# Two groups' scatters ahead of two units in a sparse-expert build stage

## The reference, cut to what matters

```python
def peer_ffn(x, w_q, sub_keys, u, v):
    ...
    s1, i1 = lax.top_k(s[..., 0, :], PEER_TOPK)
    s2, i2 = lax.top_k(s[..., 1, :], PEER_TOPK)
    ...
    cand_i = (i1[..., :, None] * PEER_NKEYS + i2[..., None, :])
    top_s, pos = lax.top_k(cand_s, PEER_TOPK)
    gate = jax.nn.softmax(top_s, axis=-1)
    ...
        hid = jnp.einsum('thkd,td->thk', u[ib], xb)
        a = jax.nn.gelu(hid.astype(jnp.float32), approximate=False) * gb
        return jnp.einsum('thk,thkd->td', a.astype(x.dtype), v[ib])
```

## Time and profile before

| | |
|---|---|
| median of 3 runs | 1659.34 us (1658.65 to 1662.34) |
| profiled execution | 1656.8 us, span 1655.0 us |
| busy in the span | PE 1623.7 (98%), PEld 1484.2 (90%), DVE 1034.1 (62%), ACT 978.3 (59%), POOL 1128.9 (68%) |
| chain that ended last | PE 85%, POOL 6%, issue 3%, DVE 3%, ACT 2%, DMA 1% |
| build stage | first scatter at 1131.74 us, late stage from 1325.68 us |

### The profile page before, as it was taken

How to read it: one execution, slowest core, us unless ns; L and a number is a source line. 1 busy time by engine, 2 the same in 40 slices (tenths; PEclk the granted TensorE clock), 3 DMA queues, 4 the chain that set the end, 5 groups by cost and what they waited for, 6 DMA issues and landing times.

```text
span 1655.0 us, 30488 instructions
## 1 busy us (share of the span) xinstructions
PE 1623.7 (98%) x10334; PEld 1484.2 (90%) x10334; DVE 1034.1 (62%) x2292; ACT 978.3 (59%) x1972; POOL 1128.9 (68%) x897
## 2 busy tenths in 40 slices
PE   8999999999999999999999999999999999999999
PEld 7888888889998888799998999988999999999998
DVE  2785432334343332746443398986999988889997
ACT  5556655556465555665653667675555566666665
POOL 8455799998989999887655699997899811111210
PEclk9999999999999999999999999999999999999999
DMA  6333455555555555554352466665777788889995
GB/s 235 102 104 113 153 188 184 187 189 168 189 166 190 190 187 186 165 174 129 130 188 90 141 199 207 203 224 196 238 250 254 249 290 284 271 303 312 333 344 174
DMA packets 104318, 334.38 MB, mean 202 GB/s; under 512 B 12144, under 2 KB 26608, under 8 KB 103952
## 3 DMA queue, kind: packets, MB, share of 16 engines
q1 hardware_dynamic: 94368, 294.99, 53.2%
q0 software_dynamic: 9696, 37.91, 7.7%
q10 hardware_dynamic: 144, 0.08, 0.0%
HBM read 324.90 MB, written 7.47 MB: 201 GB/s over the span
## 4 chain that ended last, share of the span: by engine, by line
PE 85%; POOL 6%; issue 3%; DVE 3%; ACT 2%; DMA 1%; SPq 0%; POOLq 0%; DVEq 0%; ACTq 0%
PE bank L777 21%; PE bank L809 18%; PE bank L1438 10%; PE bank L810 9%; POOL w_lo L685 6%; PE banks_and L777 6%; PE bank L1440 5%; PE banks_and L1438 3%; PE bank L1415 2%; PE banks_and L1440 2%; PE bank L755 1%; PE banks_and L1327 1%; PE banks_and L1415 1%; DMA ring<-stream 1%; ACT w_hi L1493 1%
## 5 line engine op out<-in xcount | busy, mean ns | idle before, releaser
L685 POOL TENSOR_TENSOR w_lo<-ring,w_hi 128x512 fp32r<-128x512 f32 x804 | 1041.8, 1313 | 237.7 <-ACT w_hi L1493 202.8
L1493 ACT ACTIVATE w_hi<-ring 128x512 fp32r<-128x512 f32 x1060 | 663.3, 630 | 527.8 <-PE bank L810 248.0
L809 PE MATMUL bank<-h_high_and_low,w_hi 128*128 128x448 f32 (+1 forms) x1728 | 583.5, 389 | 2.0 <-POOL w_lo L685 1.9
L810 PE MATMUL bank<-h_high_and_low,w_lo 128*128 128x224 f32 (+1 forms) x1728 | 467.5, 271 | 0.0
L809 PEld LDWEIGHTS bank<-h_high_and_low,w_hi 128*128 128x128 f32 x1728 | 325.1, 188 | 52.5 <-POOL w_lo L685 3.9
L810 PEld LDWEIGHTS bank<-h_high_and_low,w_lo 128*128 128x128 f32 x1728 | 328.8, 190 | 1.6
L1438 PE MATMUL bank<-A_high_and_low,w_hi 128*128 128x448 f32 x768 | 256.6, 375 | 1.6 <-ACT mask_parts L1968 1.6
L777 PE MATMUL bank<-h_high_and_low,w_hi 128*128 128x256 f32 x1312 | 249.1, 288 | 2.2 <-POOL w_lo L685 1.7
L777 PEld LDWEIGHTS bank<-h_high_and_low,w_hi 128*128 128x128 f32 x1312 | 209.7, 194 | 4.9 <-issue 2.6
L1440 PE MATMUL bank<-A_high_and_low,w_lo 128*128 128x224 f32 x768 | 202.0, 263 | 0.0
L2827 DVE TENSOR_TENSOR w_lo<-ring,w_hi 128x512 fp32r<-128x512 f32 x256 | 176.2, 689 | 27.5 <-ACT w_hi L1493 16.0
(11 more groups left out here) (447 smaller groups left out, 2360.5 us busy)
## 6 DMA issues: line engine op xcount, KB each, us to landing
ring<-stream SPq DMA_DIRECT2D x530, 512.0 KB, 3.6
spill<-mask_parts SPq DMA_DIRECT2D x56, 112.0 KB, 2.8
XN<-spill SPq DMA_DIRECT2D x56, 112.0 KB, 6.1
arena<-branch_w POOLq DMA_DIRECT2D x1, 3072.0 KB, 12.7
X<-x SPq DMA_DIRECT2D x2, 512.0 KB, 4.4
arena<-kv_w SPq DMA_DIRECT2D x1, 1024.0 KB, 6.0
out<-X SPq DMA_DIRECT2D x4, 256.0 KB, 2.1
arena<-row POOLq DMA_DIRECT2D x1, 512.0 KB, 4.8
```

The costliest lines, as they stand in the source:

```text
L685: nc.gpsimd.tensor_tensor(w_lo[:, hs, :], ring[:, slot(phase, e), k * HALF:(k + 1) * HALF], w_hi[:, hs, :].bitcast(F32), ALU.subtract) \
L809: mm(dst[:, 0:2 * n], high, h[:, k, :, 0:n], start=k == 0, stop=False, skip_group_check=True)
L810: last = mm(dst[:, 0:n], low, h_hi[:, k, 0:n], start=False, stop=k == KC - 1, skip_group_check=True)
L1493: A(w_hi[:, half_slot(phase, e, k), :], ring[:, slot(phase, e), k * HALF:(k + 1) * HALF], ACT.Copy).then_inc(rounded, 1)
```

## The change

On TensorE the scatters of groups g and g + 1 stand together, for every even g, then unit g and unit g + 1. On VectorE the loop takes two groups a turn: one-hots of n and n + 1, sum of unit n - 2, weigh of n - 2 and of n - 1, sum of unit n - 1, then the pick of either group. In the last turn (n = 54) the sum of unit 53 is left for behind the loop. No instruction is added or taken away, and no buffer changes. ScalarE, POOL and SP keep their code.

```diff
@@ -1418,7 +1418,9 @@
                 for i in range(BUILD_ITERS):
                     for g in range(BUILD_GROUPS):
-                        scatter(g, i)
+                        if g % 2 == 0:
+                            scatter(g, i)
+                            scatter(g + 1, i)
                         c = i * BUILD_UNITS + g
                         pe.wait_ge(*before_turn(f"build{c % 3}", c // 3))
                         feature_apart(bank(f"build{c % 3}"), "peer_build", g, i, n=T)
@@ -2806,13 +2808,19 @@
                 summed_early(2)
-                for n in range(2, GROUPS_OF_4):
+                for n in range(2, GROUPS_OF_4, 2):
                     one_hots(n)
+                    one_hots(n + 1)
+                    summed_build(n - 2)
                     weigh(n - 2)
-                    summed_build(n - 2)
-                    if n in PICK_GROUPS:
-                        pick(PICK_GROUPS.index(n))
+                    weigh(n - 1)
+                    if n + 2 < GROUPS_OF_4:
+                        summed_build(n - 1)
+                    for m in (n, n + 1):
+                        if m in PICK_GROUPS:
+                            pick(PICK_GROUPS.index(m))
                 V.memset(mx8[:], 0.0).then_inc(*frees("iota"))
+                summed_build(GROUPS_OF_4 - 3)
                 weigh(GROUPS_OF_4 - 2)
                 summed_build(GROUPS_OF_4 - 2)
                 weigh(GROUPS_OF_4 - 1)
```

## The result

The changed kernel takes 1662.38 us (median of 20 runs, 1659.66 to 1666.44) against 1659.22 (1655.74 to 1662.34): a ratio of 1.0021, interval 1.0015 to 1.0028, so 3.2 us slower. The profiled execution has a span of 1661.8 us, 6.8 above that of before. About half of this lies ahead of the change: the first scatter starts at 1135.26 instead of 1131.74. Over the twelve profiles of this study that start lies between 1131.3 and 1136.4 us, in no order that goes with the edits. One part of that is TensorE's clock: in the 12 to 13 us ahead of the first scatter the granted clock was 0.86 before and 0.78 after, and 1.00 in e5 alone. So the measure from here on is the **length of the build stage**, from the first scatter to the first product of the late stage: 1131.74 to 1325.68 is 193.94 us before, 1135.26 to 1332.49 is 197.23 after.

What follows compares the result with a forecast made beforehand. The prediction took TensorE to bound the build stage. From the profiled 1656.8 us, a 0.9 us gain at the stage's start and zero for all other terms gave 1655.9, plus 2.5 to the median: 1658.4, range 1657.0 to 1662.3.

Steps and rivals of the forecast that it cites:

- rival B: One-hots late on VectorE, so a pair's second scatter waits: +2.3 us, 1661.6, at the far bound 1663.6; chance 0.17.
- r = 8.8: Latest start of the next one-hots on VectorE, in us after a pair of scatters ends, before TensorE must wait.
- the healing after each wait: In the build stage, each wait of a scatter moves the units too, so the lag heals itself; no size given.
- VectorE: the same instructions, a later wait: Step on VectorE's build-stage queue: one-hots stay in time by 0.1 us, cost 0, bounds up to 5.2 us.
- The rule on the lock: VectorE picks with two SBUF inputs and GpSimd reading SBUF lock each other out; at its worst +3.2 us.
- The place within the run: Where scatters would wait in the build stage: the last pairs of each run of four picks, about 0.8 us each.
- Other queues: Step on ScalarE, SP, POOL and the stage's end: gelu waits 0 or 0.1 us, fetches fit in 3.4 us; taken as 0.
- The start of the stage: Scatter 3 fills TensorE's 1.56 us wait ahead of unit 2, leaving 0.7: gain 0.9 us, bounds 0.5 and 0.9.
- The switch between fp32 and fp32r: On TensorE between scatter and unit products: no cost per switch, so 56 fewer are worth 0, bounds -0.5 to +0.5 us.
- rival D: Faster: each switch of product type on TensorE costs 0.16 us, 9.0 us for 56, giving 1649.4; chance 0.04.
- Rival C: The change does nothing: unit 3's split is late or the 0.9 us is lost at the stage's end; 1659.3, chance 0.10.

Runs made afterwards that it cites:

- e5: The changed kernel with row fetches on POOL only behind the splits of odd units; 1658.34 us against 1660.15, ratio 0.9993.
- e3: The changed kernel with the pick moved ahead of the odd unit's sum on VectorE; 1661.68 us against 1658.84, ratio 1.0014.
- e4: The changed kernel with a PSUM column as second input of the 20 build-stage picks, only to measure; 1657.47 us against 1658.84, ratio 0.9989.
- e7: The kernel before with its first three fetches behind units 1, 3 and 5 instead of all behind unit 1; 1658.88 us against 1660.15, ratio 0.9993.
- e9: The kernel of e7 run again, the kernel before with its first three fetches apart; 1658.67 us against 1659.22, ratio 0.9992.

## Why the prediction was wrong, point by point

**The forecast.** 1658.4 us in a range of 1657.0 to 1662.3; measured 1662.38. What happened is rival B, which had a chance of 0.17: the second scatter of a pair waits for VectorE. Its place (the sum of the odd unit ahead of the pick), its bound of r = 8.8, and the healing after each wait were right. That its price of 3.2 us of waits, less 0.9, comes near the measured 3.2 is luck: it was reckoned as 0.8 us at the end of each of four runs of picks, and it came as 0.7 to 1.0 us in five other places. In the example above the pair of scatters at 1211.75 stands two units, 5.0 us, behind the one before it, so r is 1216.44 - 1206.75 = 9.69. That is 0.9 beyond 8.8, against a measured 0.97; and e5, where r comes to 8.8 and 8.9 in the run of turns 22 to 28, has waits of under 0.1 there.

**The step that failed is the length of a pick**, in "VectorE: the same instructions, a later wait". It took 1.72 to 2.05 us for a pick from 20 that all met POOL in the same two ways: one half running, and a gap or a fetch behind it. The rule on the lock was in the text, but its worst case was put at the longest pick of the trace. The trace of before had what was needed to take a pick apart, shown here: a pick with POOL's running half and the fetch behind it, and then the 12 picks beside the late stage, where POOL is nearly idle:

```profile
1223.42 1.85 DVE L2760 SCALAR_TENSOR_TENSOR arena<-arena 128x1024 f32<-128x1024 f32 x1
...
1222.90 1.30 POOL L685 TENSOR_TENSOR w_lo<-ring,w_hi 128x512 fp32r<-128x512 f32 x1
1224.34 1.76 POOL L697 DMA_INDIRECT arena<-u_rows,rows  x1
...
L2760 DVE SCALAR_TENSOR_TENSOR arena<-arena 128x1024 f32<-128x1024 f32 x12 | 14.6, 1219 | 0.0
```

The work alone is 1.22 us, and the pick ended 1.07 us behind the half (1225.27 and 1224.20), so some 0.6 of its 1.85 us is waiting; the fetch behind the half did not go ahead of it. So an estimate from the mechanism is 1.2 us and every half that may go first, 1.25 each. With two whole halves that is 3.7, and with an r of 6.5 + 3.7 = 10.2 the scatter would be 1.4 us late at a single pick. The picks that made scatters wait took 3.02 to 3.28 us, r came to 9.4 to 9.7, and the scatters were 0.70 to 0.97 us late. The Trainium skill has the rule ("SBUF — State Buffer", "SBUF: two separate sides": the first to start holds the shared ports for its whole instruction, the other blocks fully). The runs agree, with 3.28 beside 1.21 us; they add that POOL's next half can go ahead of the pick that already waits, two halves in a row in e3.

**The place within the run** was off for the same reason. The forecast had the wait at the fourth pick of four, by a growing lag. It came at the first of each run but the run of turns 6 and 8, where a fetch behind an even unit's split (units 12, 22, 32, 42 and 52) bunched the halves. "Other queues" let the fetch between a pair's halves pass, since POOL had 3.4 us to spare for it. For the splits that was right; what it did to the pick was not asked.

**The start of the stage**: right. Gain 0.90 us (e4: 193.94 to 193.04), the wait ahead of unit 2 0.7 us as forecast, unit 3 not late. It holds for the execution: in that of e5 the wait was 1.71. Not seen: the same wait could be had whole, 1.8 us, by moving two fetches (e7).

**The switch between fp32 and fp32r**: right, at zero. Every pair of e4's stage but the one with the wait at unit 2 takes 6.80 us, and rival D is out. Rival C too: the gain at the start was there.

**The other queues**: ScalarE's gelu waited 4.2 us in 6 places for VectorE's sums, where 0.1 was forecast; five of them, 0.7 to 1.0 us each, are for sums behind long picks and cost TensorE nothing, and the sixth, 0.3 at the end of the stage, is there before as well. No wait of TensorE for the ring, the spills or the late stage is new (1.58 us ahead of the late stage in all kernels).

## What to carry to other kernels

Where VectorE runs at 97 in 100, the length of an instruction there can't be taken from its median. For each that reads two SBUF tensors while GpSimd works on SBUF, take its length where GpSimd is idle, and add to it all that GpSimd has ready when it comes or gets ready while it waits. A change of order on TensorE also changes the rhythm in which a helper engine gets its work, two and two here instead of one by one, and that rhythm decided here. And a wait that a reordering would only fill can perhaps be removed by itself, as it was here: three fetches in a row were the whole of it (1.8 us of the stage in e7 and e9).

## What was not expected of the hardware

A VectorE pick that waits for POOL didn't get its turn between two of POOL's halves when the second had been ready for 0.37 us or more: behind the one that ran it let one more pass, in e3 two, and took 4.05 us there for 1.21 of work. With 0.13 us it did get its turn. In the other direction a fetch's issue of 0.95 us took 1.75 to 2.04 behind a pick, in the kernel before already (nine at 1.75 or 1.76). After a scatter that waited, the way to the next pair was 5.97 us for 5.90, 0.07 beyond the wait. And a stage of 190 us repeated to 0.03 us between two executions of one kernel, twice, while its start moved by 1 to 2 us and the late stage took 329.4 or 331.0 us: for an edit within a stage, the stage's length in the profile can show smaller differences than the median of the whole. It is one execution each, and e5, 1.3 us or more over what was expected, shows that what comes ahead can reach into the stage.
